# RWKV recurrence: the state chain set into the next pair's products, and the two norms in 32-column lanes

## What is computed

```python
kk = heads(k * k_k)
kk = kk / jnp.maximum(jnp.linalg.norm(kk, axis=-1, keepdims=True), 1e-12)
k = k * (1 + (a - 1) * k_a)
decay = jnp.exp(-jnp.exp(heads(w)))

def step(S, inp):
    r_t, d_t, k_t, v_t, kk_t, a_t = inp
    sk = jnp.einsum('bhvk,bhk->bhv', S, kk_t)
    S = (S * d_t[:, :, None, :] - sk[..., None] * (kk_t * a_t)[:, :, None, :]
         + v_t[..., None] * k_t[:, :, None, :])
    return S, jnp.einsum('bhvk,bhk->bhv', S, r_t)
...
mean = jnp.mean(y, axis=-1, keepdims=True)
var = jnp.mean(jnp.square(y - mean), axis=-1, keepdims=True)
y = ((y - mean) * lax.rsqrt(var + RW_GN_EPS)).reshape(b, t, d) * lnx_g + lnx_b
bonus = jnp.sum(r_h * k_h * r_k, axis=-1, keepdims=True) * v_h
out = ((y + bonus) * g) @ wo
```

## Time and profile before

| what | us |
|---|---|
| median of 3 runs | 4460.83 |
| the three runs | 4456.4, 4460.83, 4480.49 |
| the profiled execution | 4479.17 |
| its span, first to last instruction | 4477.4 |
| its mean granted TensorE clock | 0.955 |
| in it: the recurrence (`rwkv_core`), from 488.7 to 1280.3 | 791.6 |

### The profile page before, as it was taken

One profiled execution on the slowest core, in us unless ns is written; L12 is line 12 of the kernel. 1 busy time (PEld: TensorE's weight loads), 2 busy tenths in 40 slices (PEclk: granted clock), 3 DMA queues, 4 the chain that ended last, 5 costly groups with the idle time before them and its releaser, 6 DMA issues. The chain is left out here.

```text
span 4477.4 us, 77310 instructions
## 1 busy us (share of the span) xinstructions
PE 4106.1 (92%) x34672; PEld 2705.7 (60%) x34672; DVE 1530.2 (34%) x2452; ACT 840.9 (19%) x2029; POOL 134.8 (3%) x137
## 2 busy tenths in 40 slices
PE   5999788888889999999997999999937999999998
PEld 2566576667756666665564666666525666666556
DVE  5100355556514433331112345444433433333001
ACT  1000233323212111110100222222212211111000
POOL 0000000000002000000000000000001000000001
PEclk8999899889999999999998999999968999999999
DMA  1122201011020111112221111111063111111323
GB/s 62 51 75 77 68 26 31 25 33 35 10 100 1 49 35 39 39 35 78 103 104 62 46 46 35 46 46 35 27 248 149 29 36 39 36 38 33 112 96 129
DMA packets 85445, 264.75 MB, mean 59 GB/s; under 512 B 37000, under 2 KB 43528, under 8 KB 76552
## 3 DMA queue, kind: packets, MB, share of 16 engines
q1 hardware_dynamic: 85128, 259.96, 17.0%
HBM read 224.34 MB, written 35.58 MB: 58 GB/s over the span
## 5 line engine op out<-in xcount | busy, mean ns | idle before, releaser
L279 PE MATMUL ps<-sb_h,sb_w 128*128 128x384 f32 (+1 forms) x4224 | 1289.8, 468 | 1.8 <-issue 1.8
L279 PEld LDWEIGHTS ps<-sb_h,sb_w 128*128 128x128 f32 x4224 | 801.7, 190 | 485.2 <-issue 2.8
L311 PE MATMUL ps<-sb_big,sb_w 128*128 128x384 f32 (+1 forms) x2112 | 646.6, 468 | 1.2 <-ACT sb_tmp L398 1.2
L1513 PE MATMUL ps<-sb_h,sb_w 128*128 128x384 f32 (+1 forms) x1728 | 575.8, 479 | 16.2 <-DMA sb_tmp<-c_amask 13.6
L311 PEld LDWEIGHTS ps<-sb_big,sb_w 128*128 128x128 f32 x2112 | 400.2, 190 | 241.6 <-ACT sb_tmp L398 2.2
L1513 PEld LDWEIGHTS ps<-sb_h,sb_w 128*128 128x128 f32 x1728 | 316.1, 192 | 197.8 <-issue 29.3
L486 DVE COPY sb_tmp<-sb_tmp 128x2 f32<-128x2 f32 x88 | 14.9, 169 | 760.8 <-ACT sb_tmp L398 760.7
L620 PE MATMUL ps<-sb_big,sb_w 128*128 128x384 f32 (+1 forms) x768 | 234.5, 468 | 0.0
L395 ACT ACTIVATE sb_tmp<-ps 128x384 f32<-128x384 f32 x176 | 86.3, 490 | 731.7 <-PE ps L279 731.7
L417 DVE TENSOR_TENSOR sb_tmp<-sb_tmp 128x384 f32<-128x384 f32 (+1 forms) x63 | 34.8, 552 | 526.8 <-ACT sb_tmp L343 525.1
L620 PEld LDWEIGHTS ps<-sb_big,sb_w 128*128 128x128 f32 x768 | 145.8, 190 | 88.5 <-issue 0.5
(11 more groups left out here) (251 smaller groups left out, 4143.3 us busy)
## 6 DMA issues: line engine op xcount, KB each, us to landing
sb_w<-wdown SPq DMA_DIRECT2D x46, 1408.0 KB, 6.0
sb_w<-wup SPq DMA_DIRECT2D x88, 512.0 KB, 3.6
sb_w<-wqkv SPq DMA_DIRECT2D x36, 512.0 KB, 3.6
sb_big<-kT SPq DMA_DIRECT2D x8, 2304.0 KB, 12.6
sb_big<-vc SPq DMA_DIRECT2D x8, 2304.0 KB, 14.1
rkv_scratch<-sb_w SPq DMA_DIRECT2D x24, 544.0 KB, 2.7
sb_w<-wrkv SPq DMA_DIRECT2D x24, 512.0 KB, 3.5
sb_x<-xT SPq DMA_DIRECT2D x2, 4352.0 KB, 17.6
```

Source lines behind the costliest of these rows:

```text
L279: mm = pe.matmul(m.ps[:, 3 * q + b, 0:n], wt[f % 2][q][:, k, :], m.H[:, k, t0:t0 + n], start=(k == 0), stop=(k == KT - 1))
L311: mm = pe.matmul(m.ps[:, u % 6, 0:n], wdt[u % 2][:, f, :], hid[:, f, t0:t0 + n], start=(f == 0), stop=(f == FT - 1))
L1513: mm = pe.matmul(m.ps[:, ring(s, p), 0:w], wt[t][:, k, :], m.H[:, k, t0:t0 + w], start=(k == 0), stop=(k == KT - 1))
```

## The change

**The chain moves into the next pair.** Step `c` of pair `i` is now issued just before one half of a stage of pair `i + 1`: the 15 steps stand before the 15 first halves of `at`, `kq`, `rb`, `rk`, `bt`, `kt`, `vt`, `bv` (`CHAIN`). Both TensorE and DVE have the steps in that place. The chain of the last pair has no pair behind it and runs by itself at the end.

**The output is taken in two parts.** `y_local` (what a chunk gives by itself, and all of the samples' part) is made whole at the end of the pair and taken out by ACT (stage `yl`); `y_states` (32 products with the states) follows the chain as one stage `ys`, and DVE adds it in `add_states`.

**Other work is set elsewhere.** The gates are made for the next pair, not the one after it, among `rb` to `bt`; the output gate comes in two pieces after `t0` and in level 4; mean, deviation and `finish` of the pair before move into the levels and behind `y5`; `qt` moves to before `y5`, `bonus` to before `G`. `sample_states` has a semaphore of its own. `Rt` has three buffers, `Ec` and `Nc` have their own rows, and the three pairs of PSUM banks are used strictly in turn.

**The norms.** `sums` is four products, 128 rows by 32 columns of weights, of 272 moving columns each, into the four quarters of the partitions; the root and the reciprocal then work on 128x272 tiles; `spread` is four products of 32 rows by 128 columns, 272 moving columns each.

The diff, cut to its core:

```diff
+    CHAIN = {}
+    for n, st in enumerate(("at", "kq", "rb", "rk", "bt", "kt", "vt", "bv")):
+        CHAIN[st, 0], CHAIN[st, 1] = 2 * n + 1, 2 * n + 2
...
-                dve.tensor_scalar(invk, rootk, 1e-12, None, ALU.max)
+                dve.tensor_scalar(rootk, rootk, 1e-12, None, ALU.max)
                 dve.drain()
-                dve.reciprocal(invk, invk).then_inc(prep_d, 1)
+                dve.reciprocal(rootk, rootk).then_inc(prep_d, 1)
...
+            def step(i, c):
+                if c == PC - 1 and i:
+                    dve.wait_ge(out_s, 16 * i)
+                dve.wait_ge(stp, i * (PC - 1) + c)
+                dst = Sc[:, c, :] if c < PC - 1 else sout[:, 8, :]
+                dve.scalar_tensor_tensor(out=dst, in0=m.ps[:, 7, 0:HD], scalar=pend[i % 2][:, c:c + 1],
+                                         in1=Nc[:, c, :], op0=ALU.mult, op1=ALU.add).then_inc(std, 1)
...
             def mask(i, st, which, dst):
                 for half in range(2):
+                    if i and CHAIN[st, half] < PC:
+                        step(i - 1, CHAIN[st, half])
                     wait_full(dve, i, st, half)
...
-            def sums(src, bank_):
+            def sums(src):
-                for j in range(9):
-                    t0 = min(j * P, T - P)
-                    mm = pe.matmul(m.ps[:, bank_, 2 * j:2 * j + 2], src[:, t0:t0 + P], bones[:, 0:P:64], start=True, stop=True)
+                for c in range(4):
+                    mm = pe.matmul(m.ps[32 * c:32 * c + 32, 6, 0:LANE], bones[:, 48:80], src[:, c * LANE:(c + 1) * LANE], start=True, stop=True)
...
+                for half in range(2):
+                    free(i, st, half)
+                    for e in range(2):
+                        lane = slice(64 * half + 32 * e, 64 * half + 32 * e + 32)
+                        mm = pe.matmul(m.ps[:, 2 * PAIR[i, st, half] + e, 0:LANE], sel[lane, :], inv[lane, :], start=True, stop=True)
...
+            def step(i, c):
+                pe.wait_ge(std, i * STEPS + c)
+                for r in heads:
+                    mm = pe.matmul(m.ps[r, 7, 0:HD], Ec[r, c, :], Sc[r, c - 1, :], start=True, stop=True)
+                mm.then_inc(stp, 1)
...
             def chunks(i, st, parts, source, target, before=None, last=NCH):
                 for half in range(2):
+                    if i and (st, half) in CHAIN and CHAIN[st, half] < PC:
+                        step(i - 1, CHAIN[st, half])
                     free(i, st, half)
...
+                y_local(i, Rch)
+                sample_states(i)
+            out_gate(LAST, 0)
+            out_gate(LAST, 1)
+            for c in range(1, PC):
+                step(LAST, c)
+            y_states(LAST)
```

More of the change, by code:

```diff
@@ L685, in numbered @@
-    def numbered(first, before, after, end):
+        prev, ahead = i > 0, i < LAST
+        gate = [[(i + 1, "sa", g)] if ahead else [] for g in range(3)]
+        PIPE += [(i, "at"), (i, "kq"), (i, "rb")] + gate[0] + [(i, "rk")] + gate[1] + [(i, "bt")] + gate[2] + [(i, "kt"), (i, "vt"), (i, "bv")]
+        PIPE += ([(i - 1, "ys")] if prev else []) + [(i, "t0")] + ([(i - 1, "g", 0)] if prev else []) + [(i, "t1"), (i, "z0")]
+        PIPE += ([(i - 1, "mean")] if prev else []) + [(i, "x1"), (i, "t2"), (i, "z1")] + ([(i + 1, "kn")] if ahead else [])
@@ L687, in numbered @@
+    STEPS = PC
+    def numbered(first, events, end):
         order = list(first)
         for i in range(PAIRS):
-            order += [(i - 1, n) for n in before if i] + [(i, n) for n in after[0]]
-            order += [(i + 1, n) for n in after[1] if i < LAST] + [(i, n) for n in after[2]]
+            order += [(i + d, n) for d, n in events if 0 <= i + d < PAIRS]
         return {e: n + 1 for n, e in enumerate(order + end)}
-    SUMS = numbered([(0, "levels"), (0, "keys")], ["vars"], ([], ["keys"], ["W", "U"]), [(LAST, "vars")])
@@ L741, in rwkv_core @@
         Ws, Us = small(HD), small(HD)
-        rootk, invk, rootv, invv = (small(18) for _ in range(4))
+        LANE = T // 4
+        rootk, rootv = (m.lanes[:, n * LANE:(n + 1) * LANE] for n in range(2))
+        sel = small(P)
         PW0, PA0, PKK, PKA, PRK, PLG, PLB = range(7)
@@ L1023, in mask, with add_states @@
                     ins.then_inc(outd, 1)
+            def add_states(i):
+                YT = ch(YTS[i % 2])
+                wait_taken(dve, i, "yl", 1)
+                for half in range(2):
+                    wait_full(dve, i, "ys", half)
+                    dve.tensor_tensor(octet(YT, half), octet(YT, half), octet_ps(i, "ys", half), ALU.add).then_inc(outd, 1)
             def center(i):
+                YT = YTS[i % 2]
                 for half in range(2):
@@ new lines, in y_states @@
+            def y_states(i):
+                pe.wait_ge(std, i * STEPS + PC - 1)
+                wait_taken(pe, i, "RP", 1)
+                Rch = ch(Rt[i % 3])
+                for half in range(2):
+                    free(i, "ys", half)
+                    for c in range(8 * half, 8 * half + 8):
+                        bank, col0 = place(i, "ys", c)
+                        for r in heads:
+                            state = Sc[r, c - 1, :] if c else qm[r, NS:NS + C]
+                            mm = pe.matmul(m.ps[r, bank, col0:col0 + C], state, Rch[r, c, :], start=True, stop=True)
+                    mm.then_inc(full, 1)
```

439 lines of the change are left out of this document (211 added, 228 removed).

## The result

| | median us | range, runs |
|---|---|---|
| before, beside these runs | 4466.13 | 4456.4 to 4480.49, 5 |
| after | 4437.72 | 4429.65 to 4442.33, 5 |

The ratio on record is 0.992, 95% interval 0.9896 to 0.9945 (the two medians alone give 0.9936): faster, by 28 us between the medians, where 4380 us were forecast and 4435 was the end of the range. The profiled execution of after is 4442.33 us (span 4440.5), the one of before 4479.2; between these two 37 us went.

A forecast was written before the change was run, and what follows sets the result against it. It took PE's code fetch to bound the main stretch and a two-engine waiting loop the chain. Pairs falling from 94.7 to 80 us made 88 us off in all, giving 4380 us, midway between 4391 and 4373; range 4330 to 4435.

The forecast's parts named there:

- The sum: Whole pair: stretches total 78.2 us, plus 2 us, half of the earlier excess over the code-fetch floor, give 80 us.
- The chain hidden: Stages `at` to `bv`: the carried steps run among masks and evictions, 17.9 us, where stages and chain took 15 + 21.
- The slower case: Chain steps cost 2.48 us instead of 0.72, waiting behind masks and halves; pair 108 us, whole 4540 us; chance 0.04.
- From the chain to `t0` and the key sums: After the last step: `y_states`, `t0`, four output-gate products at 0.61 us each and key sums, 6.7 us.
- The norms: Sums and spread: four operations take 7.3 us of PE a pair without overlap, 1.8 if the four products overlap wholly.
- The reciprocal: On DVE, 272 columns take 1.8 us, twice a pair; PE stands about 2 us before `key_norms`.
- Levels and output norm: Levels 1 to 4 with norm work 26 us, including the 2 us stall; then `t5` to `y5` 8.0 us.
- The end: End of the pair, W to the samples' states: 305 products, 17.3 us, plus 2.3 us of waits before `E`, 19.6 us.
- Code floor: PE's instruction fetch: 64 small products make one block of at least 3.63 us; 19.6 blocks a pair, 71 us.
- floor hidden: Rival: code gaps fall under waits that are there anyway, so only waits count; 74 us a pair, 4335 us; chance 0.20.
- Clock: Sign: clock near 1.00 in the pairs, its drop left only in the bare last chain; wrong if it falls in pairs.
- The queueing rival: DVE and ACT queue up, each of five stretches loses 1 to 2 us; 87 us a pair, 4425 us; chance 0.20.

The follow-up runs named there:

- the loads apart: Changed kernel with Rt's load, the sample states' load, V's load and the state store each issued at a stage of its own (t0 to t3): 4411.69 us.
- small: Products of t1 to t5 issued twice, 170 more a pair: 4484.08 us on the kernel with the loads apart, 4493.31 us on the changed kernel.
- wide: One 128x128 by 320 column product added ahead of each half of t1 to t5: 4432.5 us on the kernel with the loads apart, 4443.78 on the changed kernel.
- late experiments: Kernel with the loads apart, with VectorE's bonus terms of the next pair moved behind level 2's mask: 4407.08 us.
- old norms: Norms of the kernel before put back: 4456.42 us in the kernel with the loads apart, 4465.96 us in the changed kernel.

## Why the prediction was wrong

**The step that failed** is in "The sum": 78.2 us by stretches and a margin of 2 us "for stalls" gave 80, with no term for the transfers. The change sends the state store, V and the sample states off together at the end of `bv`, and Kk with Rt at the pair's end; in the trace of before, Kk, Rt and V are issued at 684.7, 704.8 and 720.2, and only the store and the sample states stand together, at 716.0 and 716.4. I had taken the wait and the queue of each PE step apart, and of the DMAs only that they move. I had even named the resource that they disturb, the packets of code, and written that these would come "spread evenly, 3.6 to 4.3 us apart". Those two sentences should have met. Worth: 5.0 us a pair (88.5 to 83.5), 35 us between the profiled executions, 26 between the medians. What the runs showed in its place: where a code packet falls due inside a burst it comes about 2 us late, PE stands for it, and in two pairs of six 13.7 us at the lower clock follow.

**Step by step.**
- *The chain hidden, 17.9 us from `at` to `bv`*: right within 1 us. From the first step to the end of `bv` six pairs of after took 17.8 to 20.4 us (19.2 in pair 2), with the loads apart 17.3 to 18.2, steps 0.7 us apart at the end. The slower case, 2.48 us a step, is nowhere: L1287 waited 8.2 us for VectorE in six pairs.
- *From the chain to `t0` and the key sums, 6.7 us*: 8.4 to 8.9 us in the pairs with the loads apart, 16.3 and 16.5 in the two slow pairs of after. Too small by 2: its four gate products alone take 3.4 us (0.84 from one to the next), I had 2.4.
- *The norms, 7.3 us for four operations*: 3.6 us with the loads apart, sums of 0.67 and spreads of about 1.1, so between the two ends (1.8 and 7.3), nearer the lower. This term was too dear by 3.7 us a pair. "Tiling Modes" in the Trainium skill's page "TensorEngine Tiling (Array Packing)" gives four independent tiles and so 1.8 us; the trace agrees in part: a sum's eight records of 272 columns take 0.67 us, where by my rate they would take 1.83 without overlap and 0.46 with a whole one; a spread's take about 1.1.
- *The reciprocal, 1.8 us, and a stall of 2*: right, 1.85 us, and PE stood 2.19 us ahead of `key_norms`, for the level's mask (L1094) that VectorE takes behind the reciprocal:

```profile
724.00 1.85 DVE L990 RECIPROCAL sb_lanes<-sb_lanes 128x272 f32<-128x272 f32 x1
...
725.77 1.22 DVE L1094 TENSOR_TENSOR sb_w<-ps,sb_tmp 128x512 f32<-128x512 f32 x2
```

```profile
726.45 0.80 PE L1304 MATMUL ps<-sb_tmp,sb_big 64*64 64x64 f32 x36 [2.19 <-DVE sb_w L1094]
727.27 1.29 PE L1246 MATMUL ps<-sb_lanes,sb_tmp 32*128 32x272 f32 x8
```

- *Levels and output norm, 34 us*: 35.9 with the loads apart. *The end, 19.6*: 20.9 there, 20 to 23 in after. Each 1 to 2 us short. Together the stretches measured 83.2 us where the sum had 78.2: the norms' saving of 3.7 doesn't show in them, and the margin of 2 covered less than half of what they were short.
- *Pair 0 at 75, pair 7 at 75, the tail with its output gate at 36*: 72, then 80 (76 with the loads apart), then 38, of which the gate took 4.4.
- *Code floor, 19.6 blocks, gaps of about 1 us*: right in kind (19 to 21 fetches a pair; gaps of 0.2 to 1.9 us outside the bursts), supported by the small, wide and late experiments, and not by the old norms. Evenly spread the packets were not, even without the loads: 3.2 to 7.4 us apart. The rival "floor hidden" is out: with no later transfers at all the pairs are still 83.4 us, and 36 us of six pairs are gaps that each end 2.2 to 2.9 us behind a code packet's start. The Trainium skill's "mostly hidden" ("Runtime: NRT & Kernel Launch", "Instruction fetch mechanics") doesn't agree with this trace, by these 36 us in 501.
- *Clock*: forecast near 1.00 in the pairs. It was 0.93 to 0.98 in four pairs and 0.90 in the two with a gap of over 3 us. This sign of being wrong came true.
- *The medians*: profiled before 4479.2, median then 4460.83; I had left open whether the 18 us between them were the clock in the chains. 37 us went between the profiled executions and 28 between the medians (with before at 4466.13 now), so at most part of it was.

The sum, for the profiled executions: forecast 88 less, found 37. Of the 51 between them, 35 are the bursts; the other 16 are read from the kernel with the loads apart: 21 in six pairs (3.5 each), 4 in the last pair and the tail, less 1 in pair 0, less 3 because the recurrence of before is 757 us where my windows sum to 754, less 5 that went outside the recurrence. The queueing rival, 4425 at 87 us a pair, comes near in number and isn't the cause of the lost 5 us: PE's waits for VectorE are as long with the loads apart (42.7 us in six pairs, 43.5 in after), its gaps for code aren't.

## What to carry to other kernels

When an edit moves DMA issues, put them on a line of time beside everything else that uses the DMA engines, instruction fetch too: here three transfers of 1.1 MB together in front of dense small products cost up to 3 us of standing and a stretch at the lower clock, and setting them 6 to 9 us apart cost nothing. When PE runs many small instructions, a stall taken out elsewhere may come back as code gaps, and an optimization that lengthens a dependent step (the wide reciprocal) pays only where the order has work between its producer and its user. Test halves of a change apart before adding up their gains: here neither half by itself can be told from nothing, both together give 28 us, and with the loads apart 53.

## What the runs showed of the hardware that I had not expected

- A gap of 3.1 us in PE's work was followed, both times, by 13.7 us at the lower clock level, in the middle of dense work. Gaps of 2.2 to 2.8 us in this kernel and the one with the loads apart were followed by 3.4 or 6.8 us of it. The length of the gap alone doesn't decide: a gap of 3.81 us in the kernel with wide products (at 881.5) brought 3.4 us, one of 2.38 us in the one with old norms (at 625.1) brought 13.7. What does is open.
- Whether a burst holds PE up hangs on where it meets the code packets: with a packet started 0.9 to 1.4 us ahead of it the next came 5.8 to 6.4 us later (three pairs), with one started up to 0.9 us behind it, 3.9 to 4.1 (three pairs). Six cases are few, and no run moved the burst by such small steps.
- Three transfers begun within 0.84 us landed after 4.2, 4.6 and 4.9 us; set apart (V begins 6.1 us behind the sample states, the store 8.9 us behind V), after 4.0 (the median with Kk's), 2.7 and 2.6.
- What a stretch at the lower clock costs where code gaps stand in it: six pairs of after have 67 us of it, with the loads apart 34, with the late terms besides 14. The first step came with 5 us a pair, of which the clock, if a stretch at that level costs half its length, can be at most 2.7, the second with none. How much it was stays open, since no run changes the clock alone.
